# Sparse attention in a hybrid two-layer trunk: queries turned by one transposing DMA a head

## What is computed

```python
q = rope(rms_norm(q), pos)                      # 16 heads of 96; 4 heads share one group of keys
s_c = einsum(q, k_cmp) * scale                  # compressed branch, 31 keys
s_s = einsum(q, k_selected) * scale             # selected blocks: 512 tokens hold 8 blocks, 16 are chosen, so all
s_w = einsum(q, k_window) * scale               # window of 512 tokens, so all as well
o = gate0 * softmax(s_c) @ v_cmp + gate1 * softmax(s_s) @ v_s + gate2 * softmax(s_w) @ v_w
out = x + (o.reshape(S, H * DV) * silu(z)) @ w_out
```

## Time and profile before

| | |
|---|---|
| median of 3 runs | 868.58 us (868.13 to 869.23) |
| the profiled execution | 868.95 us |
| its span, first to last instruction | 867.2 us |
| TensorE busy | 848.3 us, 98% |
| weight loads of TensorE | 709.4 us, 82% |
| VectorE, ScalarE, GpSimd busy | 562.8, 502.0 and 485.5 us |
| DMA | 58.93 MB, mean 68 GB/s |
| the attention's loop over heads | about 679 to 814 us |

### The profile page before, as it was taken

The page is one execution under the profiler, slowest core; times in us unless marked ns, Lnnn a source line. Parts: engine busy times, 40 slices in busy tenths (PEclk is TensorE's granted clock), DMA queues, the critical chain, the costliest instruction groups (busy, mean ns, idle before and its releaser), DMA issues.

```text
span 867.2 us, 16773 instructions
## 1 busy us (share of the span) xinstructions
PE 848.3 (98%) x6041; PEld 709.4 (82%) x6041; DVE 562.8 (65%) x1607; ACT 502.0 (58%) x1151; POOL 485.5 (56%) x627
## 2 busy tenths in 40 slices
PE   6999999999999999999999999999999999999998
PEld 6999998888888888778888888778887677777786
DVE  5899988887878787653111113278689688888521
ACT  6456667887877778652134223434443789898610
POOL 2000407876767686343347424366675699999731
PEclk9999999999999999999999999999999999999999
DMA  6433322111111101122227222222233100100011
GB/s 217 131 98 98 98 79 77 39 52 51 43 28 37 53 14 50 49 97 97 96 93 134 93 92 65 80 97 74 79 97 97 50 3 2 51 3 2 2 49 49
DMA packets 39324, 58.93 MB, mean 68 GB/s; under 512 B 8757, under 2 KB 22346, under 8 KB 39242
## 3 DMA queue, kind: packets, MB, share of 16 engines
q1 hardware_dynamic: 39200, 57.85, 21.4%
q10 hardware_dynamic: 42, 0.01, 0.0%
HBM read 55.63 MB, written 2.10 MB: 67 GB/s over the span
## 4 chain that ended last, share of the span: by engine, by line
PE 85%; DVE 8%; ACT 3%; issue 2%; POOL 1%; DMA 0%; ACTq 0%; DVEq 0%; POOLq 0%
PE bank L97 19%; PE bank L99 18%; PE bank L98 18%; PE bank L1280 4%; DVE w_lo L2180 2%; PE bank L502 2%; PE bank L484 2%; PE bank L1263 2%; PE bank L511 2%; PE bank L503 2%; PE bank L1231 1%; PE bank L1232 1%; PE bank L591 1%; PE bank L592 1%; PE bank L590 1%
## 5 line engine op out<-in xcount | busy, mean ns | idle before, releaser
L2003 POOL TENSOR_TENSOR w_lo<-w_raw,w_hi 128x2048 fp32r<-128x2048 f32 (+1 forms) x26 | 118.4, 4554 | 124.0 <-ACT w_hi L1728 123.9
L97 PE MATMUL bank<-w_hi,h_hi 128*128 128x512 f32 (+3 forms) x472 | 171.4, 363 | 1.7 <-DVE h_lo L2100 1.0
L99 PE MATMUL bank<-w_hi,h_lo 128*128 128x512 f32 (+3 forms) x472 | 166.8, 353 | 0.0
L98 PE MATMUL bank<-w_lo,h_hi 128*128 128x512 f32 (+3 forms) x472 | 166.8, 353 | 0.0
L1728 ACT ACTIVATE w_hi<-w_raw 128x2048 fp32r<-128x2048 f32 (+1 forms) x26 | 49.2, 1893 | 94.0 <-PE bank L99 94.0
L97 PEld LDWEIGHTS bank<-w_hi,h_hi 128*128 128x128 f32 x472 | 88.7, 188 | 15.1 <-issue 3.4
L99 PEld LDWEIGHTS bank<-w_hi,h_lo 128*128 128x128 f32 x472 | 88.7, 188 | 11.5
L98 PEld LDWEIGHTS bank<-w_lo,h_hi 128*128 128x128 f32 x472 | 88.9, 188 | 10.1
L789 POOL TENSOR_TENSOR p<-kvr,p 128x512 f16<-128x512 f32 (+1 forms) x96 | 88.5, 942 | 10.1 <-ACT p L705 9.9
L97 PE MATMUL bank<-w_hi,o_hi 128*128 128x512 f32 x192 | 77.2, 402 | 0.8 <-DVE o_lo L2340 0.8
L99 PE MATMUL bank<-w_hi,o_lo 128*128 128x512 f32 x192 | 75.8, 395 | 0.0
(11 more groups left out here) (367 smaller groups left out, 2440.9 us busy)
## 6 DMA issues: line engine op xcount, KB each, us to landing
w_raw<-in_nsa_w_in SPq DMA_DIRECT2D x10, 1024.0 KB, 5.0
w_raw<-in_mla_w_in SPq DMA_DIRECT2D x8, 1024.0 KB, 5.2
w_raw<-in_mla_w_out SPq DMA_DIRECT2D x8, 1024.0 KB, 5.0
w_raw<-in_nsa_w_in SPq DMA_DIRECT2D x8, 984.0 KB, 5.0
w_raw<-in_nsa_w_out SPq DMA_DIRECT2D x4, 1024.0 KB, 5.1
w_raw<-in_mla_w_uq SPq DMA_DIRECT2D x7, 576.0 KB, 4.2
w_raw<-in_mla_w_ukv SPq DMA_DIRECT2D x15, 256.0 KB, 2.7
w_raw<-in_mla_w_in SPq DMA_DIRECT2D x4, 704.0 KB, 5.7
```

The source lines that it names most:

```text
L97: nc.tensor.matmul(out, a[0], b[0], start=start, stop=False)
L98: nc.tensor.matmul(out, a[0], b[1], start=False, stop=False)
L99: return nc.tensor.matmul(out, a[1], b[0], start=False, stop=stop)
L2003: nc.gpsimd.tensor_tensor(w_lo[g % 2][:, :, 0:width], w_raw[g % 2][:, :, 0:width], w_hi[g % 2][:, :, 0:width].bitcast(F32), ALU.subtract). ...
```

## The change

The queries of a head are split before they are turned. ScalarE makes the float16 high part from `qs` in SBUF, VectorE the low part, both into a buffer `q16` with the 96 dimensions padded to 128 (`q_low` and the new `high`), and one DMA with transposition, issued by SP, turns high and low parts of all four token tiles to `qT`. `q16` has two buffers (`QS`), `qT` three (`QR`). The split runs two heads ahead of its use instead of one. TensorE's transposes go, and with them the semaphore `q_turned` and the waits that guarded bank 7. The split of heads 0 and 1 moves into the projection, ahead of ScalarE's squares of the last query items, and into VectorE's table `before` at item 19. GpSimd clears the padding (`clear_pads`) after its last weight split. SP issues the first load of output weights, the DMA of head 0, the second load, the DMA of head 1; the DMAs of heads 2 to 15 stand in its order ahead of the other two loads of output weights.

```diff
-                    qT_hi = [at_slab(f"qT_hi{a}", 20 + 4 * a, [DK + 2, SEQ], F16) for a in range(2)]
-                    qT_lo = [at_slab(f"qT_lo{a}", 22 + 4 * a, [DK, SEQ], F16) for a in range(2)]
+                    QR, QS = 3, 2
+                    qT = [at_slab(f"qT{a}", 114 + 2 * a, [P, 2, SEQ], F16) for a in range(QR)]
+                    qT_hi = lambda n: qT[n % QR][0:DK + 2, 0, :]
+                    qT_lo = lambda n: qT[n % QR][0:DK, 1, :]
+                    q16 = [at_slab(f"q16_{a}", 128 + 2 * a, [P, 2, NT, P], F16) for a in range(QS)]
+                    q_head = lambda n: qs[:, :, n * DK:(n + 1) * DK]
...
+                    def turn_q(sp, n):
+
+                        if n == 0:
+                            sp.wait_ge(rows_set, 2)
+                        sp.wait_ge(q_lo, n + 1)
+                        if n:
+                            sp.wait_ge(q_landed, 16 * n)
+                        if n >= QR:
+                            sp.wait_ge(s_done, U * (n - QR + 1))
+                        sp.dma_start_transpose(qT[n % QR][:, :, :].rearrange("d s (t c) -> d (s t) c", t=NT),
+                                               q16[n % QS][:, :, :, :].rearrange("p s t d -> p (s t d)")
+                                               ).then_inc(q_landed, 16)
+
                     def sync(sp):
+                        for n in range(QS, H):
+                            turn_q(sp, n)
                         rows = nsa_w_out[0].rearrange("(k p) c -> p k c", p=P)
                         for g in range(2, 2 * OC):
...
-                        def turn_q(n):
-
-                            if n:
-                                pe.wait_ge(c_left, n)
-                            else:
                                 pe.wait_ge(kt_hi, 2 * G + 1)
                                 pe.wait_ge(kt_lo, 2 * G + 1)
-                            if n % HPG == 0:
-                                pe.wait_ge(normed1, KCMP + 1 + NT * (n // HPG + 1))
-                            for t in range(NT):
-                                last = nc.tensor.transpose(x_bank[0:DK, t * P:(t + 1) * P],
-                                                           qs[:, t, n * DK:(n + 1) * DK], ident[:, :])
-                            last.then_inc(q_turned, 1)
...
                             if u == 0:
-                                pe.wait_ge(q_hi, n + 1)
+                                pe.wait_ge(q_landed, 16 * (n + 1))
...
                                 mask(n, u)
-                                if u == 0 and n + 1 < H:
-                                    turn_q(n + 1)
...
                         def high(n):
-                            act.wait_ge(q_turned, n + 1)
-                            nc.scalar.activation(qT_hi[n % 2][0:DK, :], x_bank[0:DK, :], ACT.Copy).then_inc(q_hi, 1)
+                            if n % HPG == 0:
+                                act.wait_ge(normed1, KCMP + 1 + NT * (n // HPG + 1))
+                            if n >= QS:
+                                act.wait_ge(q_landed, 16 * (n - QS + 1))
+                            nc.scalar.activation(q16[n % QS][:, 0, :, 0:DK], q_head(n), ACT.Copy).then_inc(q_hi, 1)
...
                                 exponential(n, 0)
-                                if n + 1 < H:
-                                    high(n + 1)
+                                if n + QS < H:
+                                    high(n + QS)
                                 exponential(n, 1)
...
+                    def q_low(dve, n):
+
+                        dve.wait_ge(q_hi, n + 1)
+                        at = q16[n % QS]
+                        nc.vector.tensor_tensor(at[:, 1, :, 0:DK], q_head(n), at[:, 0, :, 0:DK],
+                                                ALU.subtract).then_inc(q_lo, 1)
...
-                        low(0)
                         for u in range(U):
                             maximum(0, u)
...
+                            if n + QS < H:
+                                q_low(dve, n + QS)
                             if more:
-                                low(n + 1)
                                 maximum(n + 1, 0)
...
+                    def clear_pads():
+                        for a in range(QS):
+                            last = nc.gpsimd.memset(q16[a][:, :, :, DK:P], 0.0)
+                        last.then_inc(rows_set, 1)
...
                         sp.dma_start(w_raw[j][:, :, :], src).then_inc(w_landed[j], 16)
+                        turn_q(sp, j)
...
-                              (7, 0, 3): turn_most, (7, 1, 3): spread_most,
-                              (NIN - 1, 0, NT - 1): turn_first_q}
+                              (7, 0, 3): turn_most, (7, 1, 3): spread_most}
...
-                                 14: [lambda n=n: square1(n) for n in range(17, 21)],
+                                 14: [lambda n=n: q_high(n) for n in range(2)] + [lambda n=n: square1(n) for n in range(17, 21)],
...
                     pool.wait_ge(kt_turned, 2 * G)
+                    clear_pads()
```

More of the change, by code:

```diff
@@ L428, in sparse_attention @@
                     ct_at, cv_at = x_bank[:, 0:P], bank[6][:, 2 * P - NT:2 * P + NT * DV]
-                    q_turned, q_hi, q_lo, rows_set = sem("q_turned1"), sem("q_hi1"), sem("q_lo1"), sem("rows_set1")
+                    q_hi, q_lo, q_landed, rows_set = (sem(n) for n in ("q_hi1", "q_lo1", "q_landed1", "rows_set1"))
                     f_done, max_done, m_turned, m_in = sem("f_done1"), sem("max_done1"), sem("m_turned1"), sem("m_in1")
@@ L501, in small_terms @@
                             dst = score_bank[(U * n + u) % 3][:, w * left:(w + 1) * left]
-                            nc.tensor.matmul(dst, kT_hi[0:DK, b, g, keys], qT_lo[a][:, j * P:], start=w == 0, stop=False)
-                            nc.tensor.matmul(dst, kT_lo[:, b, g, keys], qT_hi[a][0:DK, j * P:], start=False, stop=False)
+                            nc.tensor.matmul(dst, kT_hi[0:DK, b, g, keys], qT_lo(n)[:, j * P:], start=w == 0, stop=False)
+                            nc.tensor.matmul(dst, kT_lo[:, b, g, keys], qT_hi(n)[0:DK, j * P:], start=False, stop=False)
                         def large_term(n, u, w, b):
-                            a, g = n % 2, n // HPG
+                            g = n // HPG
                             j, keys = block_of[u][0], slice(block_of[u][0] * P, (block_of[u][0] + 1) * P)
@@ L510, in large_term @@
                             dst = score_bank[(U * n + u) % 3][:, w * left:(w + 1) * left]
-                            nc.tensor.matmul(dst, kT_hi[0:rows, b, g, keys], qT_hi[a][0:rows, j * P:], start=False, stop=False)
+                            nc.tensor.matmul(dst, kT_hi[0:rows, b, g, keys], qT_hi(n)[0:rows, j * P:], start=False, stop=False)
                         def mask(n, u):
@@ L553, in compressed_scores @@
                                 dst = x_bank[:, i * 2 * NC:(i + 1) * 2 * NC]
-                                nc.tensor.matmul(dst, qT_hi[a][0:DK, tok], kcT[:, :, n // HPG, :], start=True, stop=False)
-                                last = nc.tensor.matmul(dst[:, 0:NC], qT_lo[a][:, tok], kcT[:, 0, n // HPG, :],
+                                nc.tensor.matmul(dst, qT_hi(n)[0:DK, tok], kcT[:, :, n // HPG, :], start=True, stop=False)
+                                last = nc.tensor.matmul(dst[:, 0:NC], qT_lo(n)[:, tok], kcT[:, 0, n // HPG, :],
                                                         start=False, stop=True)
@@ L686, in attend @@
                             out_products()
-                        return (lambda: turn_q(0)), ahead, attend
+                        return ahead, attend
                     def scalar(act):
                         def high(n):
-                            act.wait_ge(q_turned, n + 1)
-                            nc.scalar.activation(qT_hi[n % 2][0:DK, :], x_bank[0:DK, :], ACT.Copy).then_inc(q_hi, 1)
+                            if n % HPG == 0:
[3 more added lines that the diff above has]
+                            nc.scalar.activation(q16[n % QS][:, 0, :, 0:DK], q_head(n), ACT.Copy).then_inc(q_hi, 1)
                         def exponential(n, u):
@@ L766, in attend @@
                                 w_high(g)
[L768 removed]
+                        return high, attend
                     def gpsimd(pool):
@@ L1447, in turn_k_cmp @@
                         nc.tensor.transpose(bank[4][0:DK, 0:P], kcmp[:, :], ident[:, :]).then_inc(kt_turned, 1)
-                    turn_first_q, ahead, attend = sparse_tensor(pe)
+                    ahead, attend = sparse_tensor(pe)
                     def turn_most():
@@ L2546, in _ @@
                     before = {0: [scale_of_scores, bias_k], 6: [half_of_factor], 4: [bias_v], 5: [half_gates], 8: [compressed], 18: [kc_low],
-                              9: [lambda: most(0), lambda: most(1)], 20: [most_of_all], 27: [scale_of_values]}
```

(1 more changed line is left out.)

32 lines of the change are left out of this document (13 added, 19 removed).

## The result

The changed kernel took 870.54 us (median of 17 runs, 869.94 to 871.99), the kernel before 868.85 (17 runs, 868.04 to 870.02): ratio 1.0021, 95% interval 1.0014 to 1.0029. It is slower by 1.7 us: the interval lies clear of 1, though barely past the 0.2% that I had named as what these runs can tell. Its profiled span is 868.7 us against 867.2, the granted clock 1.00 throughout.

What follows compares the result with a forecast made beforehand. TensorE was taken to wait for ScalarE's exponential in each head. Terms -0.43 -0.1 +0.2 +2.7 +0.7 = +3.1 us; 868.95 + 3.1 - 0.37 gives 871.7 us, range 867.6 to 878.

Steps and rivals of the forecast that it cites:

- The step that decided the sign: In each head, unit 3 waits for unit 0's exponential on ScalarE, so removing 0.43 us of transposes gains nothing.
- the case that I forecast: First transposing DMA lands in 5.0 us, TensorE waits 2.7 at head 0's first square; 870.3 to 875 us, chance 0.44.
- the rival of the short DMA: At head 0's first square, a DMA of about 3 us: wait 0 to 1.3, 868.3 to 870.0 us, chance 0.25.
- The 15 sets of transposes give nothing: Between unit 0's mask and unit 3 in the heads: 6.5 us of TensorE removed, gain nothing, the stretch staying 1.58.
- Head 0's set gives 0.43: In the projection, where TensorE is fed by itself, removing head 0's transposes saves 0.43 us.
- ScalarE gives 0.1 in head 0: In head 0, where ScalarE's chain sets the pace, its shorter float16 copy saves some 0.1 us once.
- The split ahead of the last squares delays the last weight split by 0.92 and costs 0.2: Near 642.3, two VectorE subtractions of 0.46 hold GpSimd; the last weight split ends at 666.15, price 0.2 us.
- The first DMA costs 2.7: Head 0's DMA, issued at 666.7 after the pads are cleared, lands in 5.0 us; TensorE waits 2.7 at the first square.
- The port costs 0.7 in the loop, 1.7 at most: In the loop, VectorE's two-SBUF-input subtraction and GpSimd wait out each other: 0.7 us, nothing at least, 1.7 at most.
- the ring of four: In heads 4 to 8, a head's first exponential needs GpSimd's earlier subtraction; 0.95 us of slack covers GpSimd's growing lag.
- The DMAs in the loop are hidden: In the attention, each DMA is issued a head early and has 7.4 us, which hides the 5.0 expected.

Runs made afterwards that it cites:

- e3: Changed kernel with the pads cleared early and one SBUF input in VectorE's subtraction, low parts of the queries left out: 868.34 us, ratio 0.9992 to the kernel before.
- e4: Kernel before, with the four transposes of heads 1 to 15 replaced by one short matmul, queries of these heads left out: 868.34 us, ratio 0.9996.
- e5: Kernel before, with the four transposes of heads 1 to 15 made twice: 873.87 us, ratio 1.0060.
- e1: Changed kernel with the pads cleared by GpSimd ahead of its last weight splits instead of behind them: 869.55 us, ratio 1.0008 to the kernel before.
- e2: Changed kernel with VectorE's subtraction made a comparison reading one input from PSUM, low parts of the queries left out: 868.81 us, ratio 1.0001 to the kernel before.
- e12: Changed kernel with pads cleared and values early, output-weight quarter splits late, one SBUF input in VectorE's subtraction, queries' low parts left out: 864.87 us, ratio 0.9955 to before.

## Why the prediction was right, and where its sizes were off

The sign was right and the time inside the range, 1.2 us too high (871.7 for 870.54); the change was +3.1 on record and +1.7 by the medians. The step that decided the sign held. But the case that I forecast, a first DMA of 5.0 us, did not come about: by its own last sentence the prediction falls if the DMA lands in under 3.5 us or if the period moves, and the DMA landed in 3.0 (the first in 3.2) and heads 6, 9 and 11 grew. What came about is the rival of the short DMA, to which I gave 0.25, with a port that costs more. I had ended that rival's sum at +1.4; its own terms, 0.37 without a wait and 1.3 of wait, end at +1.7. With the wait as measured, 0.92, and my sizes for all else the sum is +1.3, which I had counted as no change. That the time came out slower, and inside the forecast's own 870.3 to 875, is a DMA sized too long and a port and a split sized too small: so far the number was luck. By its own steps:

- *The 15 sets of transposes give nothing*: right. Mask to unit 3 stays at 1.58 in all heads but head 9, and e3, e4 and e5 show the same from three sides. This step hung on head 15, which has no transposes.
- *Head 0's set gives 0.43*: right (65.29 to 64.86 in e3). *ScalarE gives 0.1 in head 0*: 0.06; the period of head 0 goes from 8.90 to 8.84. Its copy fell from 0.59 to 0.52.
- *The split ahead of the last squares delays the last weight split by 0.92 and costs 0.2*: the delay was 0.94 by the mark, and the cost 0.33 (e1 against e3, 65.19 to 64.86).
- *The first DMA costs 2.7*: the mechanism was right, and this term was mis-sized. The DMA was issued when I had it, 62.76 us from the mark, but landed in 3.2 us instead of 5.0, so TensorE lost 0.92 (changed kernel against e1). I had taken a value between the spread of `v_diag` and `w1v`, both in many small pieces; the nearest in time was the plain 256 KB store at 2.0. The number of pieces was a poor guide: the changed kernel's profile has 16,896 more packets under 512 bytes (25,653 for 8,757), 1,056 for each of the 16 DMAs, about as many as `w1v` has pieces, which took 7.4 to 9.0 behind a large load. From the fixed part and the rate in the Trainium skill ("DMA: Bandwidth & Descriptors", Anatomy of one DMA, and Latency and other measured facts) I had worked out 3.0 as an estimate, and the trace agrees with it, though the first of these sections gives its fixed part for DMAs that GpSimd issues and this one is SP's.
- *The port costs 0.7 in the loop, 1.7 at most*: it cost 1.10 (e2), on the path that was named, the ring of four, for 0.73 of it in head 9. The other 0.37 came through VectorE's maxima in heads 6 and 11, where it waited 0.77 and 0.91 us, more than the 0.65 that I had taken as the most for the late heads. The Trainium skill ("SBUF — State Buffer", Who interferes with whom) names the rule; the trace agrees, with 549 ns against 977 and GpSimd's 0.40 against 0.72.
- *The DMAs in the loop are hidden*: right. They take 3.0 us, 3.5 at most in the loop, of the 7.4 that I gave them, and no first square but that of head 0 waits for one.

The sum with the measured sizes is -0.43 - 0.06 + 0.33 + 0.92 + 1.10 = +1.86, against +3.1.

## What to carry to other kernels

An operation under which another engine's latency runs is free to keep and worthless to remove. Look for a repetition without it (here the last head): if the next instruction starts no earlier, put other work under that latency first, and only then does the removal pay (8.33 to 8.28 us a head here, and 8.18 in the bound of e12). Moving an operand from PSUM to SBUF can cost more than the columns saved, when the engine that it then waits for, and holds, has no gap. And a new DMA's first use is where it shows: what its issue waits for was worth 0.92 us, and clearing the pads earlier gave that back.

## What the runs showed of the hardware

A DMA that transposes 256 KB of 16-bit numbers from SBUF to SBUF landed in 3.0 us as a rule, 4.6 at most; the longest was head 1's, issued at 669.71, behind a 1 MB load issued at 667.83. Its issue keeps SP busy for 1.23 us in most heads, which nothing waited for here. This is its group by line, with the least, median and greatest ns of one and the first and last start:

```profile
L459 SPq DMA_TRANSPOSE qT<-q x16: 1232/1233/2212, 666.4 to 795.2; - x16
```

VectorE's subtraction of 128x384 with both inputs in SBUF took from 0.55 to 1.46 us beside GpSimd, and the operation of the same shape with one input in PSUM 0.54 to 0.56. The holding goes both ways: the GpSimd operation at 641.29, which took 1.59 us before, took 2.54 beside VectorE's row of such instructions.
